# Moving weight halves by the stage that reads them, a rotary step behind a differential step, and bias rows into a scratch tile

## The reference, cut to what matters

```
first_block:   h = h + 0.5 * swiglu(rmsnorm(h), w1, w3, w2)            # ffn1, d_ff = 2816
               z = rmsnorm(h) @ w_in -> q, kc, vc, ks, vs, kw, vw, g, u
               h = h + concat(nsa_attention(...), s5_mixer(u)) @ w_out
               h = h + 0.5 * swiglu(rmsnorm(h), ...)                     # ffn2
               h = h + sigmoid(rmsnorm(h) @ w_ple_gate) * (p @ w_ple)
second_block:  for l in 0, 1:      # x and a context of 256 tokens; the context is dropped after l = 0
                 shift, scale, gate = silu(c) @ w_mod[l] + b_mod[l]      # and the same for c_ctx
                 h = rms_norm(x) * (1 + scale) + shift
                 rk rv dk dv rq rg dq dg mu mv mg mlog = h @ w_in[l]
                 o_ret  = rms_norm(bidir_retention(rope(rq), rope(rk), rv)) * silu(rg)
                 o_diff = rms_norm(diff_attend(rope(dq), rope(dk), dv)) * silu(dg)
                 o_mlp  = mu * (w_s @ layer_norm(mv) + b_s) * silu(mg)
                 y = sum over the three branches of sigmoid(mlog_b) * (o_b @ w_bo[b])
                 x = x + gate * rms_norm(y @ w_o)
```

## Time and profile before

| | |
|---|---|
| median of 3 runs | 1542.64 us (1541.95 to 1546.65) |
| the profiled execution, its own time | 1544.42 us |
| its span in the profile | 1542.7 us |
| busy: PE, PEld, DVE, ACT, POOL | 1489.7, 1323.6, 947.4, 727.9, 84.8 us |
| mean granted TensorE clock | 0.998 |
| bytes moved by DMA | 223.25 MB, mean 145 GB/s |
| `w_lo` subtractions on DVE | 347, 415.7 us, mean 1203 ns |
| `w_hi` roundings on ACT | 347, 359.9 us, mean 1038 ns |

### The profile page before, as it was taken

How to read it: one execution, slowest core, us unless ns; L and a number is a source line. 1 busy time by engine, 2 the same in 40 slices (tenths; PEclk the granted TensorE clock), 3 DMA queues, 4 the chain that set the end, 5 groups by cost and what they waited for, 6 DMA issues and landing times.

```text
span 1542.7 us, 26056 instructions
## 1 busy us (share of the span) xinstructions
PE 1489.7 (97%) x10100; PEld 1323.6 (86%) x10100; DVE 947.4 (61%) x1495; ACT 727.9 (47%) x1257; POOL 84.8 (5%) x129
## 2 busy tenths in 40 slices
PE   6999999989999999999999999999999999999997
PEld 6999989779999987787778788888878887889997
DVE  5788778676666676866654437654335635547664
ACT  5444465365444465337445363222245346556444
POOL 3800000000000000002001000000000002010000
PEclk9999999999999999999999999999999999999999
DMA  8766645426666643442121124433323332225663
GB/s 294 228 206 197 208 149 170 162 84 208 216 213 208 224 149 129 167 150 69 55 83 55 56 81 148 166 124 111 107 96 96 96 123 69 84 95 178 205 205 123
DMA packets 70889, 223.25 MB, mean 145 GB/s; under 512 B 6672, under 2 KB 21008, under 8 KB 70288
## 3 DMA queue, kind: packets, MB, share of 16 engines
q1 hardware_dynamic: 54672, 195.20, 38.6%
q10 hardware_dynamic: 16128, 26.82, 5.4%
HBM read 220.94 MB, written 1.05 MB: 144 GB/s over the span
## 4 chain that ended last, share of the span: by engine, by line
PE 82%; DVE 7%; ACT 5%; DMA 4%; issue 2%; SPq 0%; DVEq 0%; ACTq 0%
PE ps L504 69%; DMA ring<-stream 3%; PE ps L517 3%; DVE w_lo L430 2%; ACT w_hi L1265 2%; PE ps L1005 1%; PE ps L1021 1%; PE ps L1013 1%; PE ps L1089 1%; PE ps L1078 1%; PE ps L978 1%; PE ps L1058 0%; DVE area L1858 0%; PE ps L1038 0%; DVE mod_junk L1884 0%
## 5 line engine op out<-in xcount | busy, mean ns | idle before, releaser
L504 PE MATMUL ps<-hn_hi,w_hi 128*128 128x256 f32 (+1 forms) x1895 | 606.4, 320 | 15.8 <-DVE w_lo L430 6.8
L430 DVE TENSOR_TENSOR w_lo<-ring,w_hi 128x1024 fp32r<-128x1024 f32 (+1 forms) x347 | 415.7, 1203 | 298.0 <-ACT w_hi L1265 294.5
L504 PE MATMUL ps<-hn_hi,w_lo 128*128 128x256 f32 (+1 forms) x1895 | 592.2, 312 | 0.0
L504 PE MATMUL ps<-hn_lo,w_hi 128*128 128x256 f32 (+1 forms) x1895 | 591.7, 312 | 0.0
L1265 ACT ACTIVATE w_hi<-ring 128x1024 fp32r<-128x1024 f32 (+1 forms) x347 | 359.9, 1038 | 330.7 <-DMA ring<-stream 256.3
L504 PEld LDWEIGHTS ps<-hn_hi,w_hi 128*128 128x128 f32 x1895 | 361.0, 190 | 44.5 <-DVE w_lo L430 10.9
L504 PEld LDWEIGHTS ps<-hn_lo,w_hi 128*128 128x128 f32 x1895 | 361.2, 191 | 21.1 <-issue 1.0
L504 PEld LDWEIGHTS ps<-hn_hi,w_lo 128*128 128x128 f32 x1895 | 360.9, 190 | 21.3
L1334 ACT ACTIVATE area<-ps 128x512 f32<-128x512 f32 (+1 forms) x136 | 67.3, 508 | 211.9 <-PE ps L504 211.6
L504 PE MATMUL ps<-area_r,w_hi 128*128 128x256 f32 (+1 forms) x578 | 135.9, 329 | 0.7 <-ACT area L1334 0.5
L504 PEld LDWEIGHTS ps<-area_r,w_hi 128*128 128x128 f32 x578 | 96.4, 188 | 13.8 <-issue 2.8
(11 more groups left out here) (327 smaller groups left out, 1590.1 us busy)
## 6 DMA issues: line engine op xcount, KB each, us to landing
ring<-stream SPq DMA_DIRECT2D x359, 512.0 KB, 3.8
mod_at<-mod_stream ACTq DMA_DIRECT2D x24, 512.0 KB, 5.4
area<-mod_stream ACTq DMA_DIRECT2D x22, 512.0 KB, 4.8
pk<-pack ACTq DMA_DIRECT2D x1, 1610.0 KB, 7.5
pk<-pack SPq DMA_DIRECT2D x1, 1549.0 KB, 12.2
h<-x_in SPq DMA_DIRECT2D x1, 1024.0 KB, 4.8
cond_at<-cond SPq DMA_DIRECT2D x2, 512.0 KB, 14.1
mod_at<-mod_stream SPq DMA_DIRECT2D x2, 512.0 KB, 12.4
```

What stands on the lines that cost most here:

```text
L430: eng.tensor_tensor(lo[:, 0:w], raw, hi[:, 0:w].bitcast(F32), ALU.subtract).then_inc(lo_ready[who], 1)
L504: m = pe.matmul(dst, w_, x_, start=(start and n == 0), stop=(stop and n == 2), skip_group_check=True)
```

## The change

1. The ring's slots, `w_lo`'s and `w_hi`'s become 1152 words wide. Raw weights are loaded at word 128 of a slot; both halves of a unit are written `set_back(name)` words ahead of that: 48, 80 or 0, by the kind of unit and the layer. The low half is still written over the raw weights, now shifted by that much.
2. In `head_steps` a `rot` step is put behind the `diff` step of the same slot.
3. In layer 0 ACT takes `mg` 0 and 1 as plain copies and applies one Silu to both in slot 30; DVE's mixing waits for that.
4. `bsrow` is no tensor of its own any more but the memory of `mod_junk`. ACT loads the 512 words of the layer in that layer's slot 4, and DVE waits for them ahead of its first mixing. SP's load of both layers at the start is gone, and POOL waits for one DMA, not two.

```diff
+PLACE = 128
+
+def set_back(name):
+    kind, l = name[0], name[1] if len(name) > 1 else 0
+    if kind in ("ffn1", "ffn2"):
+        return 0 if l == "w2" else 48
+    if kind in ("u", "kc", "vc", "q", "ks", "kw", "pleg", "wout"):
+        return 48
+    if kind == "wbo" and l == 0:
+        return 80
+    if name in (("dk", 0, 0), ("dk", 0, 1)):
+        return 48
+    if kind in ("dq", "rq", "dg", "rg", "mu", "mg", "mlog") and l == 1:
+        return 48
+    return 0
...
 def head_steps(l):
     slots = [[] for _ in slot_units(l)]
-    for at, part in RING_ROPES[l].items():
-        slots[at].append(("rot", part))
     for hh in range(4):
         slots[4 + hh].append(("tables", hh))
     for step in range(len(DIFF[l]) + 2):
         slots[DIFF_SLOT[l] + step].append(("diff", step))
+    for at, part in RING_ROPES[l].items():
+        slots[at].append(("rot", part))
...
-        with nc.sbuf_tensor("ring", [P, RING, UW], F32) as ring:
+        with nc.sbuf_tensor("ring", [P, RING, PLACE + UW], F32) as ring:
             pass
-        w_lo = sb("w_lo", [P, RING, UW], F32R)
-        w_hi = sb("w_hi", [P, HI, UW], F32R)
-        bsrow = sb("bsrow", [P, 2 * BW])
+        w_lo = sb("w_lo", [P, RING, PLACE + UW], F32R)
+        w_hi = sb("w_hi", [P, HI, PLACE + UW], F32R)
...
         mod_junk = sb("mod_junk", [P, 2 * T], F32)
+        bsrow = mod_junk[:, :]
...
-            return w_hi[:, SPLIT[name] % HI, :], w_lo[:, UNIT[name] % RING, :]
+            at = PLACE - set_back(name)
+            return w_hi[:, SPLIT[name] % HI, at:at + UW], w_lo[:, UNIT[name] % RING, at:at + UW]
...
-            sp.dma_start(bsrow[:, :], bs_rows).then_inc(block1_loaded, 16)
...
+                    if slot == 4:
+                        act.wait_ge(s("mod_used"), (MERGE_MOD, MODS)[l])
+                        act.dma_start(bsrow, bs_rows[:, BW * l:BW * l + BW]).then_inc(block2_loaded, 16)
...
                     if part == "mg":
-                        take(name, mlpu[:, 4 + j, 0:tok], ACT.Silu, tokens=tok)
+                        if slot < STATE_SLOT[l] + len(RET[l]) + 2:
+                            take(name, mlpu[:, 4 + j, 0:tok], tokens=tok)
+                        else:
+                            if slot == len(slot_units(l)) - 2 and slot - 2 < STATE_SLOT[l] + len(RET[l]) + 2:
+                                wait_taken(act, ("mg", l, 1))
+                                act.activation(mlpu[:, 4:6, 0:tok], mlpu[:, 4:6, 0:tok], ACT.Silu).then_inc(s("gates_formed"), 1)
+                            take(name, mlpu[:, 4 + j, 0:tok], ACT.Silu, tokens=tok)
...
+                    if g == 0:
+                        dve.wait_ge(block2_loaded, 16 * l + 32)
...
-                    wait_taken(dve, ("mg", l, g))
+                    wait_taken(dve, ("mg", l, max(g, 2)))
+                    if l == 0 and g == 0:
+                        dve.wait_ge(s("gates_formed"), 1)
...
-            pool.wait_ge(block1_loaded, 32)
+            pool.wait_ge(block1_loaded, 16)
```

More of the change, by code:

```diff
@@ L426, in low_part @@
             w = UNIT_WIDTH(name)
-            raw = ring[:, UNIT[name] % RING, 0:w]
+            raw = ring[:, UNIT[name] % RING, PLACE:PLACE + w]
             hi, lo = w_parts(name)
@@ L461, in _ @@
             for u in range(RING):
-                sp.dma_start(ring[:, u, :], stream[u]).then_inc(unit_loaded[u], 16)
+                sp.dma_start(ring[:, u, PLACE:], stream[u]).then_inc(unit_loaded[u], 16)
             sp.dma_start(pk[:, width(PACK):width(PACK + PACK1)], pack[:, width(PACK):]).then_inc(block1_loaded, 16)
@@ L473, in _ @@
                     sp.wait_ge(units_multiplied, RING * r + (u + 1 - RING))
-                    sp.dma_start(ring[:, u, :], stream[RING * r + u]).then_inc(unit_loaded[u], 16)
+                    sp.dma_start(ring[:, u, PLACE:], stream[RING * r + u]).then_inc(unit_loaded[u], 16)
             for u in range(rounds * RING, NU):
                 sp.wait_ge(units_multiplied, u + 1 - RING)
-                sp.dma_start(ring[:, u % RING, :], stream[u]).then_inc(unit_loaded[u % RING], 16)
+                sp.dma_start(ring[:, u % RING, PLACE:], stream[u]).then_inc(unit_loaded[u % RING], 16)
             sp.wait_ge(resid_ready, RESID_BLOCK2 + LAYERS * KT - KT // 2)
@@ L489, in unit @@
                 pe.wait_ge(unit_loaded[u % RING], 16 * (u // RING + 1) + 16 * rounds)
-                return ring[:, u % RING, :]
+                return ring[:, u % RING, PLACE:]
             def split_unit(name, body=0):
@@ L1264, in high_part @@
                 w = UNIT_WIDTH(name)
-                act.activation(w_parts(name)[0][:, 0:w], ring[:, u % RING, 0:w], ACT.Copy).then_inc(hi_ready, 1)
+                act.activation(w_parts(name)[0][:, 0:w], ring[:, u % RING, PLACE:PLACE + w], ACT.Copy).then_inc(hi_ready, 1)
                 done[0] = n + 1
@@ L2508, in _ @@
                     biased = aux[:, 8 + g % 2, 0:tok]
+                    if g == 0:
+                        dve.wait_ge(block2_loaded, 16 * l + 32)
                     tt_(by_tile(biased), by_tile(bank(4 + g, 0, tok)),
-                        bsrow[:, BW * l + P * g:BW * l + P * g + P].unsqueeze(1).broadcast_to([P, tok // P, P]), ALU.add)\
+                        bsrow[:, P * g:P * g + P].unsqueeze(1).broadcast_to([P, tok // P, P]), ALU.add)\
                         .then_inc(s("mix_biased"), 1)
-                    wait_taken(dve, ("mg", l, g))
+                    wait_taken(dve, ("mg", l, max(g, 2)))
+                    if l == 0 and g == 0:
+                        dve.wait_ge(s("gates_formed"), 1)
                     dve.wait_ge(s("mix_biased"), n + 1)
```

## The result

The changed kernel takes 1533.57 us against 1546.06 us for the kernel before, medians of 9 runs each: a ratio of 0.9918, interval 0.9901 to 0.9936. So it is faster by 10 to 12.5 us by the medians of the two comparisons, where I forecast 22.3: right in direction, inside the range, and about half the size. On the scale of the first runs the time is 0.9918 x 1542.64 = 1530.0, which is what the rival "the slower level" gave (1530.3). Whether it is right for that rival's reason is what the experiments are about.

A forecast was written before the change was run, and what follows sets the result against it. PE was taken to bound the kernel, by matmul spacing and its pauses. Placement 17.3, rotary step 3.6 and gates 1.4 summed to 22.3 us, giving 1520.3 us from the 1542.64 median; range 1514 to 1538.

The forecast's parts named there:

- the slower level: Rival: 256-column matmuls settle at 117.6 ns, so 15.5 us become 5.5 and the time 1530.3 us; chance 0.13.
- placement does nothing: Rival: spacing belongs to the streamed tile wherever weights stand, leaving only 3.6 + 1.4 us, 1537.6 us; chance 0.12.
- Absolute place: Rival: the halves' absolute place counts and 48 back is wrong for hn, 126.1 ns, 1556.8 us; chance 0.06.
- Distance 48 costs 113.9: 256-column matmuls streaming hn, with weights moved to distance 48, would take 113.9 ns each instead of 119.7.
- ffn2 4.5: Second feed-forward block: 22 w1/w3 pairs save 0.26 us each, nearly all kept as DVE has room; 4.5 us.
- ffn1 2.6: First feed-forward block: only 12 pairs gain, as DVE sets the interval in ten others; 2.6 us.
- `mlog` 3.4: Layer 1's merge: 72 matmuls save 0.42 us, eight times; 3.4 us.
- The other 1344, 5.0: Remaining 256-column matmuls in other stages: 7.8 us at full saving, cut to 5.0 for waits and short runs.
- `wbo` of layer 0, 1.8: Layer 0's merge: 288 matmuls of 512 columns moved from distance 48 to 0 save 6.4 ns each; 1.8 us.
- Rotary step 3.6: Layer 0's slot 17: maxima ahead of rotation remove a 1.97 us PE loss and 1.7 us of low clock; 3.6 us.
- Gates 1.4: Last retention steps of layer 0: gates copied plain avoid ACT table loads and a PE wait; 1.4 us.
- DVE takes it back: Rival: both feed-forward blocks gain nothing because of DVE, leaving 15.2 us, 1527.4 us; chance 0.07.

The follow-up runs named there:

- e1: Changed kernel with halves' places varying by unit row: mlog and wbo 16 words per row, w1/w3 32, 40, 56 or 64 back; hn at 48 took 113.4 ns.
- e8: Changed kernel with layer 1's half-used wbo units loaded at 512 columns and loads from its merge on written outside SP's loop; 0.9929 of the kernel before.
- e15: Changed kernel unedited, measured again on one chip beside e13 and e14; 0.9929 of the kernel before, median 1533.6 us.
- e12: As e11 but with no halves placed, timing only; second feed-forward block 164.63 us without gaps.
- e11: Changed kernel fetching only 128 of each feed-forward modulation's 512 KB, timing only; second feed-forward block 162.87 us without gaps.
- e3: Changed kernel with no unit placed back, everything else kept; 0.9972 of the kernel before.
- e13: Changed kernel with e8's loads and each modulation loaded in two 256 KB transfers around a high half; 0.9901 of the kernel before, median 1529.0 us.
- e14: e13 with w1, w3 and layer 1's mlog 16, 48, 80, 112 words back in turn; 0.9895 of the kernel before, median 1529.3 us.
- e9: Changed kernel with w2 and layer 1's wbo 32 words back and layer 1's mlog 112 back; 0.9931 of the kernel before.

## Why the prediction was right in direction and wrong in size

- *What bounds the kernel*: right. PE's spacing and its pauses account for the time: the stretches of the table, which are cut at PE's matmuls, add up to 13.0 of the 13.3 us by which the span is shorter.
- *Distance sets the spacing*: right, and the rival "placement does nothing" is out: 0.9972 without places, 0.9918 and 0.9929 with them. "Absolute place" fell with e1. The rule that I weighed (the Trainium skill, SBUF — State Buffer, section Who interferes with whom) would have had placement at nothing, as I read it; the runs disagree by 7 to 8 us. The section speaks of engines that get in each other's way and not of the places of one engine's operands, so what fails is my reading of it.
- *Distance 48 costs 113.9*: the step that failed, "I take 113.9, nearest in shape, loop and clock". The earlier trace rows had shown a second value at this very distance and I kept it for runs behind gaps; it is the other way round: behind `w2` or `area_r` in flow `hn` settles at 117.7, and of the 16 runs of ten or more matmuls right behind a gap, in the changed kernel's two feed-forward blocks and layer 1's merge, 11 are at 113.4. That is a saving of 2.0 ns for 5.8, so for 256 columns 5.5 us instead of 15.5: the rival to which I gave 0.13. The four terms of those 15.5 us, which follow, measured 6.2 together in the changed kernel's profile.
- *ffn2 4.5*: the mean of the five profiles with these places (e8 -0.47, e15 +0.86 beside the table) is 0.7, no more than the 0.8 of the kernel without places. The level gives 1.8 (e12 less e11), and the longer gaps take 1.8 back. "DVE is busy for 106.5 of 166 us, so nearly all is kept" looked at a share and not at the loop of load, high half and low half, whose latest landings don't show. *ffn1 2.6*: 0.9 in the same five, from 0.4 to 2.0; the kernels without places lie at 1.9 longer (e3) and 1.6 shorter (e12), so what placement is worth there stays open.
- *`mlog` 3.4*: 0.6, and of that 0.5 is there without places. The level took it to 8 x 0.144 = 1.2, and the ring took back the rest; e8, with fewer bytes and earlier issues, is 1.9 us shorter than the changed kernel there.
- *The other 1344, 5.0*: 205 to 383, 549 to 640 and 1150 to 1400 us give 1.1 + 0.5 + 1.3 = 3.0 in the changed kernel's profile, the first of them between 0.0 and 2.4 in the five profiles.
- *`wbo` of layer 0, 1.8*: 1.68. *Rotary step 3.6*: 3.65, stall and clock. *Gates 1.4*: 1.49. *Bias rows 0*: layer 0's slots around slot 4 are as long as before within 0.03 us, and so is layer 1's stretch from 1150 to 1300 us in e3, where no place differs. The subtraction stayed as it was, mean 1202 ns over its 347 instructions for 1203.
- *"DVE takes it back"* was priced with the full 113.9 and would have been 1527.4; taking back does happen, but on top of the slower level, and in ffn2 it is the DMA's lateness that DVE passes on, as e11 shows. That the sum ended at the other rival's number, 1530, is part luck: that rival kept the 6.8 us of the small terms and 5.5 of the level, and the feed's share, which no case held beside it, was made up by the 1344 others, which gave more than their part of those 5.5.

## What to carry to other kernels

Where one row of a trace shows a second value for the case that a forecast rests on, price the change with both, and ask which one the new order of work will meet. A faster engine shortens the time in which a ring slot must be refilled: compare the latest landing, not the median and not the busy share, with that time before a gain in flow is booked, and look among all loads in flight for bytes that nobody reads and bursts that can be split. And an edit that takes a load out of a loop changes when it is issued: try that alone before the gain is put down to the bytes.

## What was not expected of the hardware

- Spacing of fp32 matmuls in flow: period 64 words at 512 columns (226.9 or about 233 ns), and at 256 columns 119.6 to 120.1 at distances 0 and 64, 118.6 to 118.7 at 32 and 96, and two values, about 113.4 and 117.8, at the odd multiples of 16. No distance gave less than 113.3 or 226.9 ns in a long run, 1.06 times 256 and 512 columns at 2.4 GHz.
- Which of the two values a run takes repeats from round to round in an undisturbed stretch, often changes behind a pause of 0.1 us, and depends on the runs before. The rule stays open.
- One place where the clock falls in some profiles and not in others: four matmuls of 256 columns in layer 1's state step take 1.94 us in e13's profile and 1.10 in the changed kernel's, with the same wait of 0.87 us ahead of them. The windows of both, 1360 to 1380 us, the changed kernel first:

```profile
1360.00:1380.00 20.00, 18.45 (x131) 17.25 (x132) 12.81 (x23) 12.04 (x28) 1.42 (x2) 1.00 0.30 98
```

```profile
1360.00:1380.00 20.00, 17.23 (x106) 15.50 (x106) 10.01 (x17) 9.99 (x23) 1.42 (x2) 0.91 0.25 79
```

The granted clock is 0.91 for 1.00, and the stretch that holds this place, 1300 to 1400 us of the kernel before, is 1.2 us longer than before where it was 0.85 shorter: 2 us, in e13 and e14, and 1.7 in e9. None of the kernels shows both in its profiles, so whether this goes with the kernel or with the execution isn't shown; if with the execution, it is part of why a kernel's runs differ by a few microseconds.
